# Attention scores on 64-row halves, grouped products and negated queries in a three-block fp32 kernel

## What is computed

```python
def diff_attention(q, k, v, lam):          # 4 heads, two halves c of 64 features each
    s = jnp.einsum('bqhcd,bkhcd->bhcqk', qs[0], k).astype(jnp.float32) * scale
    p = jax.nn.softmax(s, axis=-1)
    a = p[:, :, 0] - lam * p[:, :, 1]
    return jnp.einsum('bhqk,bkhe->bqhe', a.astype(v.dtype), v)

def neighbourhood_attention(...):          # 8 heads of 64 features
    s_loc = einsum(q_row, k_win) * scale + bias     # keys of x, within a window
    s_ctx = einsum(q_row, k_ctx) * scale            # keys of the context
    p = jax.nn.softmax(jnp.concatenate([s_loc, s_ctx], axis=-1), axis=-1)

def softmax_attention(q, k, v, q_rope, k_rope):  # MLA: 8 heads of 64 + 32 features
    s = einsum(q, k) + einsum(q_rope, k_rope)
    p = jax.nn.softmax(s * scale, axis=-1)
    return jnp.einsum('bhqk,bkhe->bqhe', p, v)
# MLA keys: kn = rms_norm(ckv) @ w_ukv per head; k_rope = rope(h @ w[:, 384:416]), shared by all heads
```

## Time and profile before

| | |
|---|---|
| median of 3 runs | 1938.09 us (1936.62 to 1940.97) |
| profiled execution: its own time | 1938.05 us |
| its span, first to last instruction | 1935.8 us |
| TensorE, busy | 1678.1 us (87%) |
| VectorE, busy | 610.3 us (32%) |
| ScalarE, busy | 347.6 us (18%) |
| GpSimd, busy | 57.3 us (3%) |
| mean granted TensorE clock | 0.950 |

### The profile page before, as it was taken

How to read it: one execution, slowest core, us unless ns; L and a number is a source line. 1 busy time by engine, 2 the same in 40 slices (tenths; PEclk the granted TensorE clock), 3 DMA queues, 4 the chain that set the end, 5 groups by cost and what they waited for, 6 DMA issues and landing times.

```text
span 1935.8 us, 23514 instructions
## 1 busy us (share of the span) xinstructions
PE 1678.1 (87%) x9842; PEld 863.3 (45%) x9842; DVE 610.3 (32%) x1408; ACT 347.6 (18%) x852; POOL 57.3 (3%) x55
## 2 busy tenths in 40 slices
PE   6999998999999989899999989899998665566665
PEld 3744774446444674433333323355564432232322
DVE  1267839613100873321313113140543110110102
ACT  2222136312011661100000000020431000000000
POOL 1000200200010000000000000000000000000000
PEclk9999999999999999999999999999999887887878
DMA  8512239954131003499999999930327999999996
GB/s 367 210 52 87 92 144 424 420 226 189 77 121 63 24 1 131 182 428 428 428 427 427 427 428 427 428 154 27 131 108 330 427 428 426 427 428 427 427 428 294
DMA packets 39388, 538.17 MB, mean 278 GB/s; under 512 B 4362, under 2 KB 4618, under 8 KB 6644
## 3 DMA queue, kind: packets, MB, share of 16 engines
q1 hardware_dynamic: 38148, 530.80, 65.8%
q0 software_dynamic: 1136, 5.88, 0.8%
HBM read 535.61 MB, written 1.05 MB: 277 GB/s over the span
## 4 chain that ended last, share of the span: by engine, by line
PE 61%; DMA 32%; DVE 4%; issue 1%; ACT 1%; DVEq 1%; POOL 0%; SPq 0%; POOLq 0%; ACTq 0%
PE bank L619 57%; DMA mem<-in_moe 27%; PE bank L629 3%; DMA mem<-in_ada_w 3%; DMA mem<-in_w_ada 1%; DVE mem L1492 1%; PE bank L626 1%; DVEq L1489 1%; DMA mem<-in_w_out 1%; ACT mem L2268 0%; DVE mem L2017 0%; POOL mem L2605 0%; DVE mem L1826 0%; DVE mem L1847 0%; ACT mem L2426 0%
## 5 line engine op out<-in xcount | busy, mean ns | idle before, releaser
L619 PE MATMUL bank<-mem 128*32 128x256 f32 (+10 forms) x9050 | 1572.2, 487 | 233.8 <-DMA mem<-in_moe 159.6
L619 PEld LDWEIGHTS bank<-mem 128*32 128x32 f32 (+2 forms) x9050 | 776.0, 147 | 969.1 <-issue 674.8
L2268 ACT ACTIVATE mem<-bank 128x512 f32<-128x512 f32 (+5 forms) x281 | 139.1, 505 | 1099.3 <-PE bank L619 734.5
L2017 DVE TENSOR_TENSOR mem<-mem,bank 128x512 f32<-128x512 f32 (+1 forms) x32 | 17.8, 556 | 489.3 <-PE bank L619 489.3
L629 PE MATMUL bank<-mem 128*128 128x128 f32 x760 | 121.9, 286 | 15.6 <-DVE mem L2017 5.0
L2036 DVE TENSOR_TENSOR mem<-bank,mem 32x512 f32<-32x512 f32 (+1 forms) x120 | 66.6, 555 | 209.1 <-PE bank L619 207.9
L629 PEld LDWEIGHTS bank<-mem 128*128 128x128 f32 x760 | 88.3, 146 | 83.2 <-issue 47.6
L1650 DVE SCALAR_TENSOR_TENSOR mem<-mem 128x256 f32<-128x256 f32 x160 | 86.9, 543 | 10.4 <-issue 0.9
L2605 POOL TENSOR_TENSOR mem<-mem 128x1 f32<-128x1 f32 (+5 forms) x20 | 16.0, 802 | 1375.5 <-DVE mem L1492 1375.5
L1492 DVE TENSOR_SCALAR mem<-bank,mem 128x128 f32<-128x128 f32 (+2 forms) x124 | 40.1, 394 | 39.0 <-PE bank L629 38.8
L2213 ACT ACTIVATE mem<-bank 128x256 f32<-128x256 f32 (+2 forms) x54 | 19.7, 396 | 163.6 <-PE bank L619 163.5
(11 more groups left out here) (203 smaller groups left out, 532.4 us busy)
## 6 DMA issues: line engine op xcount, KB each, us to landing
mem<-in_moe SPq DMA_DIRECT2D x190, 2048.0 KB, 34.9
mem<-in_ada_w SPq DMA_DIRECT2D x24, 2048.0 KB, 11.5
mem<-in_w_in SPq DMA_DIRECT2D x10, 2048.0 KB, 8.3
mem<-in_w_ada SPq DMA_DIRECT2D x6, 2048.0 KB, 12.1
mem<-in_even_w_in SPq DMA_DIRECT2D x6, 2048.0 KB, 8.0
mem<-in_w_out SPq DMA_DIRECT2D x4, 2048.0 KB, 9.3
mem<-in_odd_w_in SPq DMA_DIRECT2D x3, 2048.0 KB, 19.8
mem<-in_even_w_out SPq DMA_DIRECT2D x2, 2048.0 KB, 7.4
```

Source lines behind the costliest of these rows:

```text
L619: return nc.tensor.matmul(o, lhsT, rhs, start=start, stop=stop, skip_group_check=True)
L2268: took(name, S.activation(o, i, func))
```

## The change

It touches the two attentions and what feeds them.

- Queries are multiplied by the negated scale when they are evicted (`q_fm`, `nq_fm`, `cqT`); the scores are then negative, VectorE takes a minimum, and that minimum is the bias of the exponential without a further instruction. The step L1814/L1851/L2118 goes. The window bias is subtracted.
- The zero halves go. A d unit's two score products and those of two neighbouring n units contract over partitions 0 to 63 and 64 to 127 ("row halves"), with 64 rows each, one after the other, into two banks. The n units are handled in pairs by TensorE, VectorE and ScalarE; their buffers grow from three to four. GpSimd's memsets at L2640 go.
- Transposed probabilities are counted in a third counter ("turn"), and the scores of unit k + 4 are issued ahead of the transposes of unit k.
- `krope` becomes `krope_g` (8 matmuls in four column groups of 32, with partial sums), an eviction of 128 x 512 and one matmul that adds the four groups; the latter is issued after `rq1`. `kn` is computed for two heads at a time in two column groups of 64.
- MLA: scores go three units ahead; VectorE divides the probabilities by their sums before the transposes (`m_scale`: a reciprocal and a 128 x 512 multiplication per unit, on which the transposes now wait by `m_scaled`); the values are the stationary data and the transposed probabilities the moving (`m_pair`: two units in two column groups of 64, 8 matmuls of 128 columns). The result is already transposed, ScalarE copies it into `attT1` (`m_out`), and 4 of the 8 `bT` tiles go.
- Expert pieces of layer 1 in slots 3 to 6 wait for `mo7` instead of `bT0`, the one in slot 8 for `bT7` instead of `bT3`.

```diff
@@ -297,7 +297,7 @@
-    took_sem = {"dve": sem("dve_took"), "act": sem("act_took")}
+    took_sem = {"dve": sem("dve_took"), "act": sem("act_took"), "turn": sem("turned")}
@@ -479,10 +479,11 @@
-    qz = [r.take(4, TOK) for _ in range(2)]
+    q_fm = r.take(4, TOK)
+    r.take(4, TOK)
...
-    nqz = [r.take(4, TOK) for _ in range(2)]
+    nq_fm = r.take(4, TOK)
@@ -494,7 +495,7 @@
-    na_p_buf = [Region(ADA_WORK + 512 * i, 512).take(512) for i in (1, 2, 3)]
+    na_p_buf = [Region(ADA_WORK + 512 * i, 512).take(512) for i in (1, 2, 3)] + [Region(ARENA2 + 4 * TOK, 512).take(512)]
@@ -549,6 +550,7 @@
+    probs1.append(Region(XN + D, 512).take(512))
@@ -565,14 +567,16 @@
+    att_T21 += [Region(XN + at, 512).take(4, P) for at in (2 * D, 0)]
...
-    BT = (4, 5, 6, 7, 0, 1, 2, 3)
...
+    m_scaled = sem("m_scaled")
@@ -1060,12 +1064,14 @@
-        B.close(t, mm(t.ps[:, n0:TOK], qz[c][:, h, P * j:P * j + P], k_fm[:, h, n0:TOK], True, True))
+        f = slice(64 * c, 64 * c + 64)
+        B.close(t, mm(t.ps[:, n0:TOK], q_fm[f, h, P * j:P * j + P], k_fm[f, h, n0:TOK], True, True))
...
-    t = B.open(f"{tag}T{u}", "act")
+    t = B.open(f"{tag}T{u}", "turn")
@@ -1084,14 +1090,20 @@
-    j, h = u // 8, u % 8
+    j = u // 8
...
-    t = B.open(f"ns{u}", "dve" if j < 2 else "act")
-    B.close(t, mm(t.ps[:, n0:TOK], nqz[h % 2][:, h // 2, P * j:P * j + P], nk_fm[:, h // 2, n0:TOK], True, True))
+    for h in (u % 8, u % 8 + 1):
+        f = slice(64 * (h % 2), 64 * (h % 2) + 64)
+        t = B.open(f"ns{8 * j + h}", "dve" if j < 2 else "act")
+        B.close(t, mm(t.ps[:, n0:TOK], nq_fm[f, h // 2, P * j:P * j + P], nk_fm[f, h // 2, n0:TOK], True, True))
...
-    (d_scores if kind == "d" else n_scores)(u)
+    if kind == "d":
+        d_scores(u)
+    elif u % 2 == 0:
+        n_scores(u)
@@ -1103,6 +1115,8 @@
+    if k + AHEAD < len(UNITS):
+        unit_scores(k + AHEAD)
@@ -1111,9 +1125,7 @@
-        probs_T("n", u, na_p_buf[u % 3], u // 8)
-    if k + AHEAD < len(UNITS):
-        unit_scores(k + AHEAD)
+        probs_T("n", u, na_p_buf[u % 4], u // 8)
@@ -1344,8 +1356,11 @@
-    t = B.open("krope", "act")
-    B.close(t, feature_major(t, w, 384, 32, 0, TOK, p0=64))
+    t = B.open("krope_g", "act")
+    for kt in range(KT):
+        g = kt % 4
+        last = mm(t.ps[32 * g:32 * g + 32, :], w[:, kt, 384:416], hT[:, kt, :], kt < 4, kt >= 4)
+    B.close(t, last)
@@ -1353,6 +1368,9 @@
+    wait_took(pe, "krope_g")
+    t = B.open("krope", "act")
+    B.close(t, mm(t.ps[64:96, :], C("sum_r"), q_raw[0], True, True))
@@ -1386,9 +1404,11 @@
-    for h in range(8):
+    for h in range(0, 8, 2):
...
-        B.close(t, mm(t.ps[0:64, :], w[:, 0, P * h:P * h + 64], ckvT, True, True))
+        for i in range(2):
+            last = mm(t.ps[64 * i:64 * i + 64, :], w[:, 0, P * (h + i):P * (h + i) + 64], ckvT, True, True)
+        B.close(t, last)
@@ -1431,8 +1451,8 @@
-    m_scores(0)
-    m_scores(1)
+    for u in range(3):
+        m_scores(u)
@@ -1458,25 +1478,38 @@
+    def m_pair(p):
+        for u in (2 * p, 2 * p + 1):
+            wait_took(pe, f"mT{u}")
+        t = B.open(f"mo{p}", "act")
+        for b in range(4):
+            for u in (2 * p, 2 * p + 1):
+                i, h = u % 2, u % 8
+                last = mm(t.ps[64 * i:64 * i + 64, 0:P], mv_tok[:, b, 64 * h:64 * h + 64], att_T21[u % 4][:, b, :], b == 0, b == 3)
+        B.close(t, last)
...
-        if u + 2 < 16:
-            m_scores(u + 2)
-        wait_took(pe, f"ms{u}")
-        probs_T("m", u, probs1[u % 3], 0)
-        if u:
-            attend("m", u - 1, 8, 64, mv_tok, (u - 1) // 8, (u - 1) % 8, att_T21[(u - 1) % 2])
-    attend("m", 15, 8, 64, mv_tok, 1, 7, att_T21[1])
-    for kt in BT:
-        if kt == 4:
-            pe.wait_ge(att_done, 6)
-        if kt == 0:
-            wait_took(pe, "mo1")
-        t = B.open(f"bT{kt}", "dve" if kt % 2 else "act")
+        if u + 3 < 16:
+            m_scores(u + 3)
+        pe.wait_ge(m_scaled, u + 1)
+        probs_T("m", u, probs1[u % 4], 0)
+        if u and u % 2 == 0:
+            m_pair(u // 2 - 1)
+    pe.wait_ge(att_done, 6)
+    for kt in (4, 5):
+        t = B.open(f"bT{kt}", "dve")
...
-    wait_took(pe, "bT3")
-    wait_took(pe, "bT2")
+    m_pair(7)
+    for kt in (6, 7):
+        t = B.open(f"bT{kt}", "dve")
+        for j in range(2):
+            last = tr(t.ps[:, P * j:P * j + P], att1[:, j, P * kt:P * kt + P])
+        B.close(t, last)
+    wait_took(pe, "bT7")
+    wait_took(pe, "mo7")
@@ -1762,7 +1795,6 @@
-    dve.wait_ge(pool_zero, 4)
@@ -1770,11 +1802,7 @@
-    if name == "q":
-        V.tensor_tensor(qz[0][0:64, m, 0:SEQ], raw[0:64], t[0:64], ALU.add)
-        last = V.tensor_tensor(qz[1][64:128, m, 0:SEQ], raw[64:128], t[64:128], ALU.add)
-    else:
-        last = V.tensor_tensor(k_fm[:, m, 0:SEQ], raw, t, ALU.add)
+    last = V.tensor_tensor((q_fm if name == "q" else k_fm)[:, m, 0:SEQ], raw, t, ALU.add)
@@ -1809,9 +1837,8 @@
-    V.tensor_reduce(a_mx[:, i:i + 1], ps[:, n0:TOK], AX, ALU.max)
-    settle()
-    V.tensor_scalar(a_neg[:, i:i + 1], a_mx[:, i:i + 1], -NA_SCALE, None, ALU.mult).then_inc(neg_max, 1)
+    V.tensor_reduce(a_neg[:, i:i + 1], ps[:, n0:TOK], AX, ALU.min).then_inc(neg_max, 1)
@@ -1838,17 +1865,15 @@
-    i = u % 3
+    i = u % 4
...
-        V.scalar_tensor_tensor(out=s[:, 0:SEQ], in0=ps[:, 0:SEQ], scalar=NA_SCALE, in1=na_bias[:, h, P - P * j:P - P * j + SEQ], op0=ALU.mult, op1=ALU.add)
-        took(f"ns{u}", V.tensor_scalar(s[:, SEQ:TOK], ps[:, SEQ:TOK], NA_SCALE, None, ALU.mult))
+        V.tensor_tensor(s[:, 0:SEQ], ps[:, 0:SEQ], na_bias[:, h, P - P * j:P - P * j + SEQ], ALU.subtract)
+        took(f"ns{u}", V.tensor_copy(s[:, SEQ:TOK], ps[:, SEQ:TOK]))
...
-        V.tensor_reduce(n_mx[:, i:i + 1], s, AX, ALU.max)
+        V.tensor_reduce(n_neg[:, i:i + 1], s, AX, ALU.min).then_inc(na_neg, 1)
...
-        V.tensor_reduce(n_mx[:, i:i + 1], ps[:, SEQ:TOK], AX, ALU.max)
-    settle()
-    V.tensor_scalar(n_neg[:, i:i + 1], n_mx[:, i:i + 1], -1.0 if j < 2 else -NA_SCALE, None, ALU.mult).then_inc(na_neg, 1)
+        V.tensor_reduce(n_neg[:, i:i + 1], ps[:, SEQ:TOK], AX, ALU.min).then_inc(na_neg, 1)
@@ -1868,7 +1893,11 @@
-    (d_max if kind == "d" else n_max)(u)
+    if kind == "d":
+        d_max(u)
+    elif u % 2 == 0:
+        n_max(u)
+        n_max(u + 1)
@@ -2107,21 +2136,21 @@
-        took(f"cqT{m}", V.tensor_scalar(cqT[:, m, :], ps[:, 0:SEQ], G("q_norm")[:, m:m + 1], None, ALU.mult))
+        took(f"cqT{m}", V.tensor_scalar(cqT[:, m, :], ps[:, 0:SEQ], G("q_norm")[:, m:m + 1], -MLA_SCALE, ALU.mult, ALU.mult))
...
-        i = u % 3
+        i = u % 4
...
-        V.tensor_reduce(m_mx[:, i:i + 1], ps[:, :], AX, ALU.max)
+        V.tensor_reduce(m_ng[:, i:i + 1], ps[:, :], AX, ALU.min).then_inc(m_neg, 1)
+    def m_scale(u):
+        wait_took(dve, f"ms{u}")
+        V.reciprocal(m_rec[:, u:u + 1], m_sum[:, u:u + 1])
...
-        V.tensor_scalar(m_ng[:, i:i + 1], m_mx[:, i:i + 1], -MLA_SCALE, None, ALU.mult).then_inc(m_neg, 1)
-    def m_norm(name, j):
-        ps = arrive(dve, name)
-        V.reciprocal(m_rec[:, 8 * j:8 * j + 8], m_sum[:, 8 * j:8 * j + 8])
-        settle()
-        took(name, V.tensor_tensor(by_head(att1[:, j, 0:512]), by_head(ps[:, :]), m_rec[:, 8 * j:8 * j + 8].unsqueeze(2).to_broadcast([P, 8, 64]), ALU.mult))
+        V.tensor_scalar(probs1[u % 4], probs1[u % 4], m_rec[:, u:u + 1], None, ALU.mult).then_inc(m_scaled, 1)
@@ -2178,20 +2206,20 @@
+    m_scale(0)
...
-        if u + 2 < 16:
+        if u + 3 < 16:
...
-            if u == 9:
-                m_norm("mo0", 0)
-            m_max(u + 2)
+            m_max(u + 3)
+        if u + 1 < 16:
+            m_scale(u + 1)
...
-    m_norm("mo1", 1)
-    for kt in BT[1::2]:
+    for kt in range(4, 8):
@@ -2385,13 +2413,9 @@
-    act.wait_ge(pool_zero, 4)
...
-        for i in range(2):
-            copy(qz[0][0:64, 2 * h + i, SEQ:TOK], ps[0:64, SEQ * i:SEQ * i + SEQ])
-            last = copy(qz[1][64:128, 2 * h + i, SEQ:TOK], ps[64:128, SEQ * i:SEQ * i + SEQ])
-        took(f"qc{h}", last)
+        took(f"qc{h}", S.activation(q_fm[:, 2 * h:2 * h + 2, SEQ:TOK], ps.rearrange("p (m t) -> p m t", t=SEQ), ACT.Copy, scale=-NA_SCALE))
@@ -2403,13 +2427,12 @@
-    take(f"{name}{m}", rope_raw[m % 2][:, 0:SEQ], ps[:, 0:SEQ])
+    took(f"{name}{m}", S.activation(rope_raw[m % 2][:, 0:SEQ], ps[:, 0:SEQ], ACT.Copy, scale=-NA_SCALE if name == "q" else 1.0))
...
-    copy(nqz[0][0:64, m, :], ps[0:64, :])
-    take(f"nq{m}", nqz[1][64:128, m, :], ps[64:128, :])
+    took(f"nq{m}", S.activation(nq_fm[:, m, :], ps[:, :], ACT.Copy, scale=-NA_SCALE))
@@ -2423,7 +2446,7 @@
-    took(name, S.activation(probs[u % 2][c][:, n0:TOK], ps[:, n0:TOK], ACT.Exp, bias=a_neg[:, i:i + 1], scale=NA_SCALE, accum_out=a_sum[:, i:i + 1]))
+    took(name, S.activation(probs[u % 2][c][:, n0:TOK], ps[:, n0:TOK], ACT.Exp, bias=a_neg[:, i:i + 1], scale=-1.0, accum_out=a_sum[:, i:i + 1]))
@@ -2431,18 +2454,22 @@
```

(51 more changed lines are left out.)

10 lines of the change are left out of this document (5 added, 5 removed).

## The result

The changed kernel takes **1925.88 us** (median of 6 runs, 1923.05 to 1930.01), the one before 1939.34 in the same comparison (6 runs, 1936.62 to 1943.19): a ratio of 0.9925, with a 95% interval from 0.9913 to 0.9938. Forecast were 1910.7 us and a gain of 27.4; the gain is 13.5 between the medians and 10.5 between the profiled spans, 1935.8 and 1925.3.

What follows compares the result with a forecast made beforehand. TensorE was taken to bound the attentions and DMA the expert streams that start behind them. Gains of 13.6 (even attention), 3.8 (`krope`), 3.0 (`kn`) and 7.0 (MLA) summed to 27.4: 1938.05 to 1910.7 us, range 1900 to 1926.

Steps and rivals of the forecast that it cites:

- the clock line in slice 13: Even attention: a drop of the granted clock line in slices 13 or 14 was named as showing the prediction wrong.
- Rival D: Expert streams: part of the gain is hidden there, half of it left, 1924 us; chance 0.06.
- The pair, 1.19: Even attention, 512 keys: two score products on row halves take 1.19 us, between 0.86 ideal and 1.72 in turn.
- Rivals A: Even attention: row halves don't overlap, gain 15.4 in all, 1922.7 us; chance 0.20.
- B (0.86, VectorE sets the pace): Even attention: a pair costs 0.86 and VectorE sets the pace, 1902.8 us; chance 0.16.
- 512 keys, 8.5: Even attention: two pairs replace four products, 1.06 us less per triple, 8.5 us over 8 triples.
- Start, 1.5: Start of the even attention: waits behind the first transposes shrink, gain 1.5 us (0 to 3).
- 256 keys, 3.6: Even attention: triples fall from 4.2 to 3.6 us, mostly by issuing scores ahead of transposes; gain 3.6 us.
- `kn`, 3.0: Ahead of MLA: `kn` in two column groups gains 3.0 us, part possibly a wait for ScalarE; ends 0 and 3.4.
- MLA, 7: MLA: less TensorE work per unit, 1 us added for coupling, `project_out` at 1432 not 1439.3; gain 7, ends 2 and 9.
- rival C: MLA: the division sets the pace, a unit takes 2.6 us instead of 1.9, 1921.9 us; chance 0.07.
- Rival E, the clock: Even attention: TensorE gets 1.2 GHz instead of 2.4 over the 512 keys, 1961 us; chance 0.06.

Runs made afterwards that it cites:

- run with fillers: Changed kernel plus three idle 128 x 512 products ahead of the even attention's first transposes; even stage 104.84 us, changed kernel 104.90.
- the four profiles at full clock: Changed kernel with `kn` one by one, `kn` to VectorE, no division, or two fixes together; unit 12 to unit 24 took 26.78 or 26.79 us.
- the run with the division first: Changed kernel with VectorE dividing MLA unit u+1 before the minimum of unit u+3; 1922.41 us, ratio 0.9901 against the kernel before.
- the five runs on other stages: Changed kernel with `kn` one by one, `kn` to VectorE, no division, division first, or two fixes together; even stages 104.8, 104.8, 106.9, 104.2, 104.2 us.

## Why the prediction was right in its direction and twice too large

The sign, the mechanism and the price of a pair held. What failed were the terms in which TensorE's saving was taken as the stage's. The time, 1925.88, lies 0.1 us inside the stated range of 1900 to 1926 and outside of the forecast's own, 1906 to 1917: it lies in the part that was there for the rivals, and of the signs named against the prediction one, the clock line in slice 13, was seen. That it lies inside by so little is luck.

- **Both streams move with the attentions: right.** 548.0 and 548.2 us for the experts of layer 0, 496.5 and 497.0 behind the odd `project_out`. Rival D is refuted.
- **The pair, 1.19: right**, 1.21 and 1.26. The Trainium skill's rule ("TensorEngine Tiling (Array Packing)", Key Properties: a change of the tiling mode drains TensorE) agrees with the runs: 2.00 to 2.05 on 64 rows against 1.77 on 128, where nothing overlaps. Rivals A (no overlap) and B (0.86, VectorE sets the pace) are refuted.
- **512 keys, 8.5: wrong, 2.5 measured** (unit 3 to unit 24, seven of the eight triples, 7.4 of the 8.5). The triple was mis-sized by a little (1.06 less forecast, 0.78 measured, 2.0 in seven; 0.14 to 0.19 of each is a wait for ScalarE's eviction that the sum didn't have, as it checked VectorE's rate and never ScalarE's place). A wait for an eviction of 0.41 is new too. Larger is what I left out: that the pairing puts a second minimum ahead of the norm of the heads, so that TensorE waits 2.06 for it and not 0.59 (a loss of 1.5), and that the clock fell behind it (28.36 us where 26.78 is taken at full clock, 1.6). That is 5.5; of it 0.57 came back, as two waits of before (0.36 and 0.21) went.
- **Start, 1.5: wrong, -0.4 measured** up to unit 3. The waits did not shrink. TensorE was done earlier, VectorE was not, so it waited 3.29 in one piece and then ran at 1.2 GHz for some 6.8 us (the shares of 0.75, 0.50 and 0.87 in the three rows are 1.5, 4 and 1.3 us at half). The run with fillers shows 1.2 us for it; in the other profiles with the same start it was 2.0 to 2.7.
- **256 keys, 3.6: the rate right, the gain not: 1.3** (unit 24 to unit 42). The rate was 3.58 as forecast, but the two waits for the norm (0.83 each, before 0.40 and 0.58) are not in it. And the reason was wrong: with scores behind the transposes it is 3.56 too. The tail, which I kept as it was, gave 1.8. VectorE asks GpSimd there for the roots that the differential heads' norm needs, and waits 2.42 us for them in both kernels (before, then after):

```profile
719.60 0.69 DVE L1867 TENSOR_TENSOR mem<-mem 128x512 f32<-128x512 f32 x1 [2.42 <-POOL mem L2605]
...
717.07 0.69 DVE L1892 TENSOR_TENSOR mem<-mem 128x512 f32<-128x512 f32 x1 [2.42 <-POOL mem L2639]
```

But it now asks 1.5 us earlier, counted from the transposes of unit 42 (1.68 us ahead of them, 0.15 before): the score and the minimum of unit 44 come together with those of unit 43, where VectorE waited 0.40 for that score. Another 0.3 is the scaling step that went. This is read from the rows; no run changes it.
- **`krope`, 3.8: right**, 3.5.
- **`kn`, 3.0: too large.** 1.76 was measured by undoing it, inside the named ends of 0 and 3.4; most of the rest is the 1.41 wait for ScalarE that the text had as possible and priced at 0.1.
- **MLA, 7: mechanism named as rival C, its size between.** 3.1 measured; from the first transposes to `project_out` it is 33.88, where about 31 was named. The sum has a slip: 1400.7 + 0.9 + 25.3 + 1 is 1427.9 and not 1428.6, so its own terms give a gain of 8.4. TensorE's own work was sized well: without the division the stretch is 7.9 us shorter than before. The 1 us that I added for coupling should have been 4.8, of which 3.25 are the order on VectorE's queue. Busy time (20.3 in 38.6 us) was the wrong evidence against C; the order of VectorE's queue was there to read.
- **Rival E, the clock, came true in small.** I gave it as all or nothing, over all 512 keys. It fell twice, for 6.8 us and for 3.4 (0.66 over 5 us), and cost 1.2 us (against the run with fillers) and 1.6 (against the four profiles at full clock). In the profile of the run with the division first it cost 2.0 and 2.9: that is why its even stage took 106.9. With such costs taken off, by the same two marks, the even stage is 101.9 to 102.1 in the changed kernel and in the five runs on other stages: an estimate of 8 us for what the change gives there at full clock, where 5.3 were measured and 13.6 forecast. Slower than before, as E had it, would have taken 31 us of such work.

Open is when a wait of this kind costs the clock. Three kernels with the same even attention have the same wait for the norm. Behind it twelve records took 2.22 us (`kn` one by one), 3.46 (the changed kernel) and 2.64 (division first), and in the last the next twelve were slow as well, 3.81 where 2.06 is usual:

```profile
667.96 2.64 PE L623 MATMUL bank<-mem 128*128 128x128 f32 x12 [2.07 <-DVE mem L1884]
...
671.43 3.81 PE L623 MATMUL bank<-mem 128*128 128x64 f32 x12
```

The Trainium skill ("TensorE: Matmul & The Clock Gate", Part 1) says that the number of slow products differs between runs of one kernel, and says it of a kernel's start; these numbers show the like in the middle of one.

## What to carry to other kernels

When a change makes the busiest engine faster, price the stage by what the next engines have *queued ahead* of what it waits for, not by their busy shares: here the pair cost what was forecast, and over half of the even attention's gain went into waits for VectorE and ScalarE and the clock behind them. A wait added by a change costs what stands ahead of its signal; look whether anything there waits for the waiting engine itself, and turn those two around first. And a wait that grows on TensorE can cost as much again in granted clock behind it: 1.6 us here behind a wait of 2.06, and 0 to 2.9 in other profiles of the same code. So compare two kernels over stretches in which the clock was the same before a difference is put down to an edit.

## What the runs showed of the hardware

- Two products of 64 rows on different row halves, issued whole and one after the other between products of 128 rows, overlap in 0.74 to 0.84 of 0.86 us; issuing them in halves and in turns changes nothing.
- Going from 128 rows to 64 and back cost 0.23 to 0.28 us a pair, and 0.05 at the transposes behind.
- A wait of 3.29 us was followed by some 6.8 us at a granted clock of 0.50, and waits of 2.20 and 1.77 close together by a clock of 0.50 too. Waits of 1.24 and 1.91, with the transposes and scores of two units between them, were not, nor 0.51 and 1.56 with fillers.
- The same wait of 2.07 us in the same code was followed by work at full clock in some profiles and by up to 2.9 us of loss in others.
- ScalarE evicted 64x512 in 0.59 us and 128x512 in 0.60.
